# The first block's mixer: high parts ahead of the softmax's exponentials, a low part inside VectorE's wait, three output tiles begun together, and two swaps

## What is computed

```python
u = rmsnorm(x, mix_norm[l])
c_q, c_kv, k_r, hq, hf, hi, hgate, mq, gate_logits = split_sizes(u @ w_in[l], IN_SPLITS)
y_mla = mla_branch(c_q, c_kv, k_r, ...) @ w_o_mla[l]          # 8 heads, causal softmax
y_hg = hgrn2_branch(hq, hf, hi, hgate, lbs[l], ...) @ w_o_hg[l]  # gated recurrence
y_mem = memory_branch(mq, mem_n, w_mem_kv[l]) @ w_o_mem[l]      # 4 heads, softmax over a memory
gates = jax.nn.sigmoid(gate_logits.reshape(B, S, N_BRANCH, D))
merged = gates[:, :, 0] * y_mla + gates[:, :, 1] * y_hg + gates[:, :, 2] * y_mem
x = x + merged @ w_out[l]
```

## Time and profile before

| | us |
|---|---|
| median of 3 runs (lowest, highest) | 2355.51 (2355.39, 2357.04) |
| the profiled execution, its own time | 2356.44 |
| its span, first to last instruction | 2354.6 |
| TensorE busy | 2334.2 (99%) |
| VectorE busy | 1639.7 (70%) |
| ScalarE busy | 1277.3 (54%) |
| GpSimd busy | 348.3 (15%) |
| mean granted TensorE clock | 0.998 of full speed |

### The profile page before, as it was taken

How to read it: one execution, slowest core, us unless ns; L and a number is a source line. 1 busy time by engine, 2 the same in 40 slices (tenths; PEclk the granted TensorE clock), 3 DMA queues, 4 the chain that set the end, 5 groups by cost and what they waited for, 6 DMA issues and landing times.

```text
span 2354.6 us, 50717 instructions
## 1 busy us (share of the span) xinstructions
PE 2334.2 (99%) x21742; PEld 2276.2 (97%) x21742; DVE 1639.7 (70%) x2270; ACT 1277.3 (54%) x1828; POOL 348.3 (15%) x296
## 2 busy tenths in 40 slices
PE   9999999999999999999999999999999999999998
PEld 9999999999999999999999999989999999989998
DVE  7865787966677657878666766776765766776763
ACT  6644656654455456565455554636554554646554
POOL 3012020300200210203003002431002002431001
PEclk9999999999999999999999999999999999999999
DMA  6555433455555544335555555422545555422543
GB/s 257 200 192 196 177 126 128 180 210 184 197 194 188 195 179 182 122 140 183 198 195 182 223 180 197 168 81 91 215 179 197 197 182 195 173 75 92 217 181 122
DMA packets 57681, 410.21 MB, mean 174 GB/s; under 512 B 6385, under 2 KB 6641, under 8 KB 8689
## 3 DMA queue, kind: packets, MB, share of 16 engines
q1 hardware_dynamic: 56304, 401.50, 46.1%
q10 hardware_dynamic: 1152, 5.46, 0.6%
HBM read 405.89 MB, written 1.05 MB: 173 GB/s over the span
## 4 chain that ended last, share of the span: by engine, by line
PE 84%; DVE 7%; ACT 4%; issue 4%; POOL 1%; DMA 0%; DVEq 0%; ACTq 0%; POOLq 0%
PE bank L558 84%; DVE sb_wlo L514 3%; DVE area L1862 1%; ACT sb_whi L506 1%; PE bank L2210 1%; ACT area L1582 0%; DVE area L1845 0%; DVE area L1811 0%; DVE area L648 0%; POOL sb_x_ssq L701 0%; ACT area L1648 0%; DVE area L1919 0%; ACT area L1606 0%; POOL area L839 0%; ACT area L1603 0%
## 5 line engine op out<-in xcount | busy, mean ns | idle before, releaser
L558 PE MATMUL bank<-area,sb_whi 128*128 128x256 f32 x11752 | 2019.1, 278 | 4.2 <-ACT sb_whi L506 1.7
L558 PEld LDWEIGHTS bank<-area,sb_whi 128*128 128x128 f32 x11752 | 1769.9, 188 | 14.5 <-issue 4.2
L558 PE MATMUL bank<-area,sb_wlo 128*128 128x256 f32 x5876 | 1607.6, 277 | 3.5 <-DVE sb_wlo L514 3.4
L506 ACT ACTIVATE sb_whi<-sb_raw 128x1024 fp32r<-128x1024 f32 x762 | 792.7, 1055 | 597.6 <-PE bank L558 585.1
L558 PEld LDWEIGHTS bank<-area,sb_wlo 128*128 128x128 f32 x5876 | 1096.1, 188 | 5.7 <-DVE sb_wlo L514 5.5
L514 DVE TENSOR_TENSOR sb_wlo<-sb_raw,sb_whi 128x1024 fp32r<-128x1024 f32 x762 | 955.0, 1264 | 158.1 <-ACT sb_whi L506 156.3
L648 DVE TENSOR_TENSOR area<-bank,sb_x_diag 128x512 f32<-128x512 f32 x244 | 167.1, 685 | 72.3 <-PE bank L558 49.7
L999 DVE TENSOR_TENSOR area<-area,area 128x256 f32<-128x256 f32 x176 | 75.8, 431 | 186.2 <-ACT area L950 185.1
L558 PE MATMUL bank<-area,area 64*64 64x64 f32 (+5 forms) x2864 | 149.5, 248 | 0.1
L558 PEld LDWEIGHTS bank<-area,area 64*64 64x64 f32 (+3 forms) x2864 | 127.2, 139 | 19.3 <-ACT area L1630 5.3
L693 POOL TENSOR_TENSOR sb_x_ssq<-sb_x 128x256 f32<-128x256 f32 x9 | 12.0, 1332 | 849.7 <-DVE sb_x L1043 839.5
(11 more groups left out here) (272 smaller groups left out, 1176.8 us busy)
## 6 DMA issues: line engine op xcount, KB each, us to landing
sb_raw<-stream SPq DMA_DIRECT2D x379, 1024.0 KB, 4.8
sb_raw<-stream SPq DMA_DIRECT2D x3, 512.0 KB, 8.0
area<-lora ACTq DMA_DIRECT2D x2, 768.0 KB, 6.4
area<-c ACTq DMA_DIRECT2D x1, 1504.0 KB, 7.2
sb_x<-x SPq DMA_DIRECT2D x4, 256.0 KB, 5.7
area<-mem ACTq DMA_DIRECT2D x1, 1024.0 KB, 7.2
out<-sb_x SPq DMA_DIRECT2D x4, 256.0 KB, 2.9
sb_raw<-stream ACTq DMA_DIRECT2D x1, 512.0 KB, 4.5
```

The source lines that it names most:

```text
L506: e.activation(k.hi[k.slot[p]], raw_piece(k, p), ACT.Copy).then_inc(*k.done("weights_hi", p))
L558: return e.matmul(out, lhsT, rhs, start=start, stop=stop, skip_group_check=True, tile_position=at)
```

## The change

In `scalar_attend`, heads 0 to 11: the two high parts stand ahead of the exponentials in place of behind the recurrence. In `vector_attend`, one of the two low parts of a head stands between the bias and the wait for the exponentials. At h = 13 `scaled_pair` stands ahead of the wait for y. `AHEAD1` is (3, (6, 2)) in place of (2, (6, 2)): three output tiles are begun together, the stream's order with it, and the parts made ahead are three pieces. In `scalar_mix1` one high part comes ahead of the copy of the recurrence's values, and in `vector_merge` the low part ahead of x's low part.

```diff
-AHEAD1 = (2, (6, 2))
+AHEAD1 = (3, (6, 2))
@@ scalar_mix1
-    hi_parts(e, k, 3 * PIECE)
+    hi_parts(e, k, 4 * PIECE)
     copied_rows(e, k, ("hg_values", s), m.vh, k.sx.tm)
-    hi_parts(e, k, PIECE)
@@ scalar_attend
         if h < HEADS:
+            hi_parts(e, k, 2 * PIECE)
             scalar_exponentials(e, k, s, m, h)
...
         scalar_recurrence(e, k, s, m, h)
-        if h <= HEADS:
+        if h == HEADS:
             hi_parts(e, k, 2 * PIECE)
-        if h == HEADS:
@@ scalar_merge
-    hi_parts(e, k, 2 * PIECE)
+    hi_parts(e, k, AHEAD1[0] * PIECE)
     for j in range(NX):
-        if j >= 2:
+        if j >= AHEAD1[0]:
             hi_parts(e, k, PIECE)
@@ vector_softmax
         *k.done("biases", s, h))
+    lo_parts(e, k, PIECE)
     e.wait_ge(*k.when("exponentials", s, h))
@@ vector_attend
             vector_softmax(e, k, s, m, h)
+        name, i, dst = fillers[h]
+        if h > HEADS:
+            scaled_pair(e, k, ("projected", s, name, i), dst)
...
-        name, i, dst = fillers[h]
-        scaled_pair(e, k, ("projected", s, name, i), dst)
+        if h <= HEADS:
+            scaled_pair(e, k, ("projected", s, name, i), dst)
         if h < HEADS:
-            lo_parts(e, k, 2 * PIECE)
+            lo_parts(e, k, PIECE)
@@ vector_merge
-    lo_parts(e, k, 2 * PIECE)
+    lo_parts(e, k, AHEAD1[0] * PIECE)
     for j in range(NX):
+        if j >= AHEAD1[0]:
+            lo_parts(e, k, PIECE)
         if j >= 2:
-            lo_parts(e, k, PIECE)
             x_low(e, k, s, j - 2)
```

## The result

| | before | after |
|---|---|---|
| median, us | 2355.99 (2355.39 to 2357.04, 5 runs) | 2374.89 (2374.45 to 2376.10, 5 runs) |
| profiled execution, us | 2356.44 | 2374.45 |
| its span, us | 2354.6 | 2372.6 |
| ratio of the times | | 1.008 (95%: 1.0069 to 1.0091) |

A forecast was written before the change was run, and what follows sets the result against it. TensorE, busy 2334.2 of 2354.6 us, bounds the kernel: only its stops and matmul rate count. Seed slot 16.0, low part -3.8 and three tiles +0.6 sum to +12.8 us, 2368.3 from 2355.5; range 2359 to 2376.

The forecast's parts named there:

- The seed slot: Attention, odd heads: ScalarE's second high part waits for the seed slot, holding the exponentials; 8.0 us per mixer, +16.0.
- only the weights bind: Rival, attention: late exponentials stop TensorE only for the scaled weights, 3.0 us per mixer; 2358.3, chance 0.09.
- The low part: Attention: VectorE's low part inside its wait for the exponentials removes TensorE's stops for low parts; -3.8 us.
- The swap at head 13: Merge: scaling the last gate pair first puts TensorE 0.5 to 0.8 us ahead, which the output tiles take back.
- The price of the three tiles: Output tiles: start waits for the third tile's bank, partly repaid by no later stops and quicker matmuls; +0.3 per mixer, +0.6.
- the clock falls: Rival: TensorE's stop of about 3 us ahead of the output tiles lowers its clock; +6.8, 2375.1, chance 0.05.
- Nothing stops behind it: Output tiles: after the later start with three tiles, TensorE has no further stops.
- kept fast: Output tiles: without a stop matmuls keep the quick rate; 0.64 us on six pieces, 0.2 on the next two.
- The high part ahead of the values' copy: ScalarE in the mixer: this reordering only moves work between instructions that have idle time; 0.
- lateness that reaches the even heads: Attention, upper bound: half of a stop more for each of the four pairs, 11.6 us per mixer.

The follow-up runs named there:

- experiment 3: The changed kernel with each head's second high part, at odd heads the seed slot's, put back behind the recurrence: 2356.82 us.
- experiment 4: The changed kernel with the seeds of the attention and the merge one piece later, the order on every engine unchanged: 2358.39 us.
- three_tiles: The kernel before with only three output tiles begun together and the parts that go with it: 2360.37 us.
- seeds_by_one: The run of experiment 4: the changed kernel with the seeds of the attention and the merge one piece later: 2358.39 us.
- one_high: The run of experiment 3: the changed kernel with each head's second high part back behind the recurrence: 2356.82 us.
- lo_inside: The kernel before with only one of VectorE's low parts moved inside its wait for the exponentials: 2352.30 us.
- experiment 7: The kernel before with only the high part ahead of the values' copy and the gate pair ahead of y's low part from head 13: 2354.99 us.
- hi_ahead: The kernel before with only ScalarE's two high parts moved ahead of the exponentials: 2382.84 us.
- bank_late: The changed kernel with each output tile's bank taken just ahead of that tile's first matmul: 2367.17 us.
- small_swaps: The run of experiment 7: the kernel before with the two swaps alone: 2354.99 us.
- experiments 8 to 10: On the kernel before, low part inside wait and both swaps; two add three tiles with late third bank, one of these an earlier low part: 2350.73, 2350.69, 2351.54.
- experiments 11 and 12: Two kernels of experiments 8 to 10 (two tiles; three tiles with the earlier low part), with GpSimd making the merge's eight sums: 2349.61 and 2349.16 us.

## Why the prediction held, and where it was off

- **The seed slot: right, and shown.** Experiments 3 and 4 take only that wait away, one by order and one by slot, and the attention falls from 104.89 to 96.38 and 97.11 us. The size was right as well: pairs of 18.93, 18.75 and 18.71 us against 18.8, the attention +13.2 against +12.2, stops at blocks 2, 4, 6 and 8. The levels of the last three stop for 1.5, 1.3 and 1.1 us, which with the 0.3 at the turn is 1.8, 1.6 and 1.4 against three times 1.8. Of its parts, head 1 was misplaced: the stop came at the turn (1.73 us) and only 0.3 at the level, while the working had the level at 2.0. The sum is the same, since the weights and the operands are late together. The rival in which only the weights bind is out.
- **The low part: right.** -3.8 forecast, -3.83 measured with it alone. Its working was a little off on both sides: block 8 has no longer work of its own (blocks 5 to 8 fall to 33.97 us, not 34.2), and block 10 takes 0.2 us more a mixer.
- **The swap at head 13: right.** 0.9 and 0.6 us ahead, all taken back.
- **The price of the three tiles: the step that failed.** Forecast +0.3 a mixer, measured +3.14 and +3.64. The stop itself was as worked out: 2.63 from the rows, and 2.7 and 3.0 in three_tiles (2.85 and 3.16 between two matmul starts, less the usual 0.12); with the swap ahead of it 3.6 in the changed kernel. Where the clock didn't fall (seeds_by_one, which also has its seeds one piece later) the stretch was 66.16 in place of 65.33, +0.8. The other 2.3 and 2.8 us come with the fall of the clock. The sum had no term for it: it was left to the rival "the clock falls", which gave 2375.1 and had a chance of 0.05, where the forecast had 0.74. It is what happened. The chance was taken from the attention's stops, of 0.6 us and less, which left the clock alone, and the text itself said that no stop of 3 us stood in the trace. The clock fell behind seven of eight such stops, so 0.05 was far too low. The rival's price, 3.4 us a mixer on top of the 0.3, was too high: 2.3 and 2.8. That its 2375.1 lies 0.2 us from the measured 2374.89 is luck in part: by the spans its +19.6 stands against 18.0, with the clock and the mixer's middle 1.7 us too high each, and the attention and the three tiles' own cost 1.0 too low each.
- **"Nothing stops behind it" was right, "kept fast" only in part**: the last six pieces take 16.96 us in the changed kernel's first mixer and 16.32 in its second; 16.32 in seeds_by_one's second mixer, where the clock stays up, and 16.96 in both mixers of one_high and three_tiles. Nor is it the stops that set the rate, as the prediction had it: in lo_inside, where nothing stops the attention, the second piece of block 4 runs at 118 ns a matmul and that of block 5 at 113.
- **The high part ahead of the values' copy: predicted 0, was -1.7 for both mixers.** It was put down as work moved between instructions with idle time. ScalarE had some, but not there: behind the values' copy stand the keys' copies, and TensorE goes on when the first of them ends (experiment 7). The wait was in the trace under the name "issue", which hid it from a reading by releaser.

So the 5.2 us between the 12.8 forecast and the 18.0 of the spans are +6.2 at the output tiles, -1.7 in the mixer's middle, +1.0 in the attention and -0.3 elsewhere. That the time lies inside the range, 1.1 us below its upper end, is luck in part: this end stood for lateness that reaches the even heads, not for the clock.

What stays open is why the last stretch is 65.29 to 65.38 us in both mixers of eight kernels (before, hi_ahead, lo_inside, bank_late, small_swaps and experiments 8 to 10). That VectorE's queue holds it is supported by the releasers of the stops there (VectorE, or ScalarE's high half of a merged tile, which itself waits for VectorE's sum) and by experiments 11 and 12; which chain of its instructions sets the number was not isolated. Why the clock fell behind one stop and not behind its like isn't settled either.

## What to carry to other kernels

A producer moved ahead in an in-order queue takes its wait for a free buffer with it, and everything that it passes then waits for that too: before moving it, look up for each instance which use frees its buffer, since one slot whose turn comes at another spacing is enough. A cover that makes a stop shorter behind can make one ahead: asking for all banks first turned a wait with work in front of it into one with none. And when a stop goes and the end doesn't move, add up the whole stretch between two fixed points, not the waits: 65.3 to 65.4 us in eight kernels said that taking one stop away only made room for the next.

## What the runs showed of the hardware

TensorE's clock fell behind seven of the eight stops of 2.9 to 3.8 us ahead of output tiles (the changed kernel, one_high, three_tiles and seeds_by_one, two each), to 0.50 of full speed for 3 to 7 us. In three of the seven it fell while TensorE still stood: in the changed kernel's second mixer it is at 0.50 from 1095.36 us on, and the first matmul comes at 1096.16. Behind the stops of 1.2 to 1.9 us in the attention it stayed at 1.00 in the changed kernel, but it fell once in bank_late (a window from 956.40 to 959.60 us, at 0.50) and once in hi_ahead (6.9 us at 0.51, above), so a shorter stop is no guarantee. The Trainium skill, TensorE: Matmul & The Clock Gate, "HAM oscillation — how this bites in real kernels", says that idle gaps bring the clock down, and the runs agree.

The matmuls' two rates, one start every 113 or every 118 ns, both stand at a granted clock of 1.00. Behind six of the seven falls the last six output pieces ran at the slow rate (16.96 us), behind the seventh, the changed kernel's second mixer, at the quick one (16.32). They ran at the slow rate before as well, without a fall, and single pieces of lo_inside's attention do so without a stop. What chooses the rate isn't settled by these runs.
